# Retention states as 128x128 blocks of two heads, results as one run of whole-array matmuls into one bank

## The reference, cut to what matters

```
result[t] = (decay_matrix * (q[t] k[t]^T)) v[t]                     within the chunk, both directions
          + (decay_0 * q[t]) state[0, before t]                     what earlier chunks left
          + (decay_1 * q[t]) state[1, after t]                      what later chunks left
state[e, next] = decay_e^128 * state[e, this] + k[t]^T (weight_e * v[t])
```

## Time and profile before

| | us |
|---|---|
| median of three runs | 2710.48 |
| lowest and highest | 2708.75, 2711.12 |
| the profiled execution, by its own time | 2710.8 |
| its span in the trace | 2709.0 |
| what lies around the span | 1.8 |

### The profile page before, as it was taken

The page is one execution under the profiler, slowest core; times in us unless marked ns, Lnnn a source line. Parts: engine busy times, 40 slices in busy tenths (PEclk is TensorE's granted clock), DMA queues, the critical chain, the costliest instruction groups (busy, mean ns, idle before and its releaser), DMA issues.

```text
span 2709.0 us, 30075 instructions
## 1 busy us (share of the span) xinstructions
PE 2497.3 (92%) x12526; PEld 1757.2 (65%) x12526; DVE 1150.0 (42%) x1966; ACT 694.4 (26%) x1218; POOL 145.4 (5%) x136
## 2 busy tenths in 40 slices
PE   7987979999999998889899999999998999799997
PEld 6873433333446987735788888876756654588886
DVE  3246331211544675725243343344265473354444
ACT  2235011111222243314211211213244352312222
POOL 0000011111022003300000000000000000000000
PEclk9988979999997798999899999999999999899999
DMA  9944469997411110031111221211100100222231
GB/s 356 337 141 128 177 241 378 336 364 297 154 33 48 32 32 1 1 140 47 47 63 47 78 63 47 78 63 49 63 16 1 63 1 31 78 78 94 93 100 72
DMA packets 178791, 302.48 MB, mean 112 GB/s; under 512 B 17963, under 2 KB 89307, under 8 KB 178528
## 3 DMA queue, kind: packets, MB, share of 16 engines
q1 hardware_dynamic: 167760, 278.46, 29.7%
q0 software_dynamic: 10320, 20.00, 2.1%
q10 hardware_dynamic: 576, 2.10, 0.2%
HBM read 348.75 MB, written 18.87 MB: 136 GB/s over the span
## 4 chain that ended last, share of the span: by engine, by line
PE 52%; DVE 8%; ACT 4%; issue 2%; DVEq 0%; ACTq 0%
PE PS L135 44%; PE PS L141 4%; PE PS L147 2%; PE PS L2727 2%; DVE R L113 1%; DVE sm L116 1%; DVE X L105 1%; DVE MIX L105 1%; ACT R L125 1%; DVE rest L105 1%; DVE H L105 0%; ACT ATb L128 0%; DVE hn L105 0%; ACT ATb L125 0%; DVE sil L110 0%
## 5 line engine op out<-in xcount | busy, mean ns | idle before, releaser
L135 PE MATMUL PS<-at,wH 128*128 128x512 f32 (+1 forms) x2112 | 567.9, 357 | 4.7 <-DVE at L105 4.7
L135 PEld LDWEIGHTS PS<-at,wH 128*128 128x128 f32 x2112 | 378.2, 191 | 64.0 <-issue 7.2
L135 PE MATMUL PS<-at,rest 128*128 128x512 f32 (+1 forms) x1056 | 375.9, 356 | 0.0
L135 PE MATMUL PS<-wH,ac 128*128 128x512 f32 x880 | 278.9, 395 | 8.9 <-issue 3.9
L105 DVE TENSOR_TENSOR rest<-ring,wH 128x2048 fp32r<-128x2048 f32 x66 | 150.4, 2291 | 242.7 <-ACT wH L128 242.2
L135 PE MATMUL PS<-ring,AT 128*128 128x512 f32 x512 | 229.0, 606 | 1.7 <-ACT AT L128 1.7
L135 PEld LDWEIGHTS PS<-at,rest 128*128 128x128 f32 x1056 | 201.1, 190 | 28.4
L128 ACT CAST wH<-ring 128x2048 fp32r<-128x2048 f32 x66 | 124.7, 1906 | 316.4 <-PE PS L135 230.4
L135 PEld LDWEIGHTS PS<-wH,ac 128*128 128x128 f32 x880 | 167.3, 190 | 46.3 <-issue 8.6
L135 PEld LDWEIGHTS PS<-ring,AT 128*128 128x128 f32 x512 | 98.2, 194 | 121.3 <-issue 119.0
L135 PE MATMUL PS<-rest,ac 128*128 128x512 f32 x440 | 172.9, 393 | 0.0
(11 more groups left out here) (324 smaller groups left out, 3857.4 us busy)
## 6 DMA issues: line engine op xcount, KB each, us to landing
R<-in_w_gate_up_dram SPq DMA_DIRECT2D x32, 1024.0 KB, 12.0
ring<-in_w_down_dram SPq DMA_DIRECT2D x32, 1024.0 KB, 12.7
ring<-in_w_gate_up_dram SPq DMA_DIRECT2D x32, 1024.0 KB
ring<-in_w_ffn_gate_dram SPq DMA_DIRECT2D x22, 1024.0 KB, 5.5
ring<-in_w_ffn_up_dram SPq DMA_DIRECT2D x22, 1024.0 KB, 5.4
ring<-in_w_ffn_down_dram SPq DMA_DIRECT2D x22, 1024.0 KB, 4.9
ring<-in_w_ada_dram SPq DMA_DIRECT2D x16, 1024.0 KB, 6.8
HIw<-in_w_gate_up_dram SPq DMA_DIRECT2D x16, 1024.0 KB, 8.2
```

The lines of the kernel that those rows point to most:

```text
L135: ins = self.e.matmul(out, l, r, start=k == 0, stop=k == len(pairs) - 1)
```

## The change

- The states of a direction now alternate between two places (256 columns each), and each state is also spread by ACT into a block form (blocks): 128 partitions by 512 columns, where column block g of 128 columns is a 128x128 matrix with head 2g in its upper left, head 2g + 1 in its lower right, and zeros elsewhere. The function expand does that with two casts of 64 partitions by 256 columns for each state, and raises "expanded".
- POOL writes the zeros beforehand with three fills: three times 512 columns of MIX, 2048 columns of the ring's slot 2, and 1536 of its slot 1, each raising "zeros". The first two stand ahead of its work on q, the third ahead of the third chunk of it.
- result(i) issues its 8 matmuls of W with v in one run, and then for each direction 4 matmuls with the whole 128x128 weights of decayed q and 128 columns of blocks. All go into one bank. It waits for "expanded" instead of "state_r".
- ACT copies a result with one cast of 512 columns. The eight high parts are no longer all at the start: two come after four states are spread, two after six, two after each of the first two result copies. The first weight piece is cast after the third result copy instead of the second.
- DVE waits, before it overwrites a state's place, until that place's earlier state is spread.
- SP issues the pieces RET + 2 and RET + 3, whose slots now hold blocks, only after the last result (y_r 6).

```diff
@@ qkv_pool
+        g.wait_ge(S("dt_raw"), 2)
+        g.up(g.e.memset(MIX[:, 1024:4096].rearrange("p (t d) -> p t d", t=3)[:, :, 512:1024], 0.0), S("zeros"))
+        g.up(g.e.memset(ring[:, 4096:6144], 0.0), S("zeros"))
+
         for i, t in enumerate(YS):
             g.wait_ge(S("qk6_copy"), 8)
+            if i == 2:
+                g.wait_ge(S("proj6"), 18)
+                g.up(g.e.memset(ring[:, 2048:3584], 0.0), S("zeros"))
             if 2 <= i < 4:
                 g.wait_ge(S("kv_r"), i - 1)
@@
-    RAW_AT, Y_AT = (3, 4), ((2, 5), (6, 7))
+    RAW_AT, Y_AT = (3, 4), (2, 6)
...
     def state(e, n):
-        q = 5 * e + n
-        Z, a_ = (X, 5632 + 256 * (q - 8)) if q > 7 else (MIX, 1024 * (1, 2, 0, 3)[q // 2] + 512 + 256 * (q % 2))
-        return Z[:, a_:a_ + 256]
+        Z, a_ = ((X, 5632), (MIX, 512))[e]
+        return Z[:, a_ + 256 * (n % 2):a_ + 256 * (n % 2) + 256].rearrange("p (g d) -> p g d", g=4)
+
+    def blocks(e, n):
+        q = after_state(e, n) - 1
+        Z, a_ = (MIX, 1536 + 1024 * q) if q < 3 else (ring, 4096 + 512 * (q - 3)) if q < 7 else (ring, 2048 + 512 * (q - 7))
+        return Z[:, a_:a_ + 512]
@@ ret_pe, result(i)
-            p.wait_ge(S("state_r"), max(after_state(e, Y_STATE[e][t]) for e in ways))
-            for g in range(4):
-                outs = [bk(Y_AT[i % 2][j], 64, 64 * g) for j in range(2)]
-                for j in range(2):
-                    h = 2 * g + j
-                    p.e.matmul(outs[j], W[:, 128 * h:128 * h + 128], rv[:, t, 64 * h:64 * h + 64], start=True, stop=False)
-                for e in ways:
-                    for j in range(2):
-                        rs = slice(64 * j, 64 * j + 64)
-                        ins = p.e.matmul(outs[j], q_by(i, e)[rs, g, :], state(e, Y_STATE[e][t])[rs, 64 * g:64 * g + 64],
-                                         start=False, stop=e == ways[-1])
+            p.wait_ge(S("expanded"), max(after_state(e, Y_STATE[e][t]) for e in ways))
+            b = Y_AT[i % 2]
+
+            for h in range(8):
+                p.e.matmul(bk(b, 64, 64 * h), W[:, 128 * h:128 * h + 128], rv[:, t, 64 * h:64 * h + 64], start=h == 0, stop=False)
+            for e in ways:
+                for g in range(4):
+                    ins = p.e.matmul(bk(b, 128, 128 * g), q_by(i, e)[:, g, :], blocks(e, Y_STATE[e][t])[:, 128 * g:128 * g + 128],
+                                     start=False, stop=e == ways[-1] and g == 3)
@@ ret_act
+        def expand(a_, b_):
+            for s_ in range(a_, b_):
+                e, n, i = STATES[s_]
+                a.wait_ge(S("state_r"), s_ + 1)
+                a.wait_ge(S("zeros"), 1 if s_ < 3 else 2 if s_ < 7 else 3)
+                for j in range(2):
+                    rs = slice(64 * j, 64 * j + 64)
+                    a.cast(blocks(e, n)[rs, :].rearrange("p (g j d) -> p g j d", g=4, j=2)[:, :, j, :], state(e, n)[rs, :, :],
+                           inc=S("expanded") if j else None)
...
-        for k in range(8):
-            a.cast(aH[:, k, :], aT[:, k, :], inc=S("a_high"))
+        expand(0, 4)
+        split(0, 2)
+        expand(4, 6)
+        split(2, 4)
+        expand(6, 10)
         for i in range(6):
             copied(i)
-            if i == 1:
+            if i < 2:
+                split(4 + 2 * i, 6 + 2 * i)
+            if i == 2:
                 a.wait_ge(S("kv_r"), 6)
                 high(a, RET)
@@ ret_dve, states
+                if n > 1:
+                    v.wait_ge(S("expanded"), after_state(e, n - 2))
@@ sync
+            elif n in (RET + 2, RET + 3):
+                fetch(s, n, (S("y_r"), 6))
```

More of the change, by code:

```diff
@@ L1836, in copied, with split @@
             a.wait_ge(S("y_r"), i + 1)
-            for j in range(2):
-                a.cast(mx[:, t, 0:512].rearrange("p (g j d) -> p g j d", g=4, j=2)[:, :, j, :], bk(Y_AT[i % 2][j], 256).rearrange("p (g d) -> p g d", g=4),
-                       inc=S("y_copy_r") if j else None)
+            a.cast(mx[:, t, 0:512], bk(Y_AT[i % 2]), inc=S("y_copy_r"))
+        def expand(a_, b_):
[7 more added lines that the diff above has]
+                           inc=S("expanded") if j else None)
+        def split(a_, b_):
+            for k in range(a_, b_):
+                a.cast(aH[:, k, :], aT[:, k, :], inc=S("a_high"))
         a.wait_ge(S("params"), 128)
@@ L1857, in states @@
                 e, n, i = STATES[s_]
-                new, kv = (x.rearrange("p (g d) -> p g d", g=4) for x in (state(e, n), state(e, n)))
-                kv = bk(i % 2).rearrange("p (g e d) -> p g e d", g=4, e=2)[:, :, e, :]
+                kv = bk(i % 2).rearrange("p (g e d) -> p e g d", g=4, e=2)[:, e, :, :]
+                new = state(e, n)
+                if n > 1:
+                    v.wait_ge(S("expanded"), after_state(e, n - 2))
                 if n:
                     v.settle()
-                    v.tt(new, state(e, n - 1).rearrange("p (g d) -> p g d", g=4), bc(ET2[:, 4 * e:4 * e + 4], 64), ALU.mult)
+                    v.tt(new, state(e, n - 1), bc(ET2[:, 4 * e:4 * e + 4], 64), ALU.mult)
                 v.wait_ge(S("kv_r"), i + 1)
```

## The result

| | us |
|---|---|
| before, median of four runs | 2710.8 (2708.75 to 2713.47) |
| after, median of four runs | 2682.9 (2682.56 to 2685.82) |
| ratio, with its 95% interval | 0.9899 (0.9882 to 0.9916) |
| predicted | 2683.5, range 2679.0 to 2692.5 |
| the profiled execution after: its time, its span | 2682.56, 2679.7 |

A forecast was written before the change was run, and what follows sets the result against it. PE was taken to bound the retention results stage, at half clock. From the profiled execution, 2710.8 - 27.7 + 0.2 (POOL's fills) + 0.2 (one more hand-over) = 2683.5 us; range 2679.0 to 2692.5.

The forecast's parts named there:

- The bound: Retention's results, 856 to 905 us: PE busy 48.2 of 49 us at clock 0.50, no other engine near.
- The clock: In the new results PE's clock stays at 1.00, as in the state space stage from 1082 to 1142 us.
- a clock that stays low or goes up and down: Results stage: clock stays at 0.50, only 8.0 us gained, 2702.8 us (7%); up and down lies between (4%).
- The sum of the stage: New results and raw runs: 23.5 us plus 0.3 for turns, 23.8 us; last result ends 27.7 us earlier.
- the turn around a raw run: Into and out of each raw run between results: 0.04 x 8 = 0.3 us, bounds 0 and 1.3 us.
- my two losses of 0.2 us: POOL's third fill slowing DVE's last rotations, 0.2 us, and one more hand-over at the end, 0.2 us.
- clock changes in later stages: After retention: an us or so each way for where clock changes fall.
- DVE in the stage: Results stage: scores 1.29 us, low parts through at about 874.8, before PE ends at 876.4; costs nothing.
- ACT: Spreading states: two casts of at most 0.33 us each, 6.5 us for ten states; nothing is late.
- POOL: Three zero fills of 1.4, 1.8 and 1.4 us; the third, at about 838 us, costs 0.2 us.
- SP: RET + 2 and RET + 3 fetched from 876.4, landed by about 888; cast at 898 to 900, hidden.
- What I did not count: Projections behind the results shrink some 2.7 us at full clock, but become PE idle time behind DVE's chain.

The follow-up runs named there:

- e1_wide: The kernel before, with W's matmuls moving 128 columns instead of 64 (not for the last head), the added ones never read: 2690.9 us, ratio 0.9936.
- e5_cols16: The changed kernel with every result matmul moving 16 columns instead of 64 and 128: 2700.7 us, ratio 0.9966.
- e4_cols64: The changed kernel with the block matmuls moving 64 of their 128 columns: 2682.5 us, ratio 0.9905.
- e7_early: The changed kernel with the second weight piece's cast and low part moved ahead of the last result: 2680.4 us, ratio 0.9883; repeated, 2679.2 us.
- e2_runs: The kernel before with only the order changed, W's 8 matmuls first, then each direction's half-row matmuls: 2682.6 us, ratio 0.9909.
- e3_pairs: The changed kernel with the old order back, head pair by head pair, blocks kept: 2678.8 us, ratio 0.9898.

## Why the prediction was right

- **The bound** was right: PE, at 0.50 of its clock, in the stage of the results.
- **The clock** was right, and by the right mechanism as far as it went. The forecast took it from the nearest rows and left 11% for a clock that stays low or goes up and down. e1_wide and e5_cols16 showed what stood behind it. The forecast gave two reasons, no alternation and 128 columns over all rows in the second half. Neither is needed by itself: e1_wide has the alternation and e4_cols64 has 64 columns, both at 1.00. The Trainium skill's rule (TensorE: Matmul & The Clock Gate, the table of why this matters), to keep TensorE continuously busy, does not cover this case: 38.0 of 38 us busy at 0.50 in e5_cols16, 31.4 of 32 busy at 1.00 in e1_wide.
- **The sum of the stage** was 1.3 us too small: 23.8 forecast, 25.1 measured (873.23 + 2.00 - 850.17), and it lies above the forecast's own upper bound of 23.5 + 1.3 = 24.8. About half of the miss is the turn around a raw run. It was taken as 0.04 us, eight times. By the runs of this stage it is 0.11 out of one (852.01 - 850.17 = 1.84, against 873.23 - 871.50 = 1.73 behind a block run) and 0.09 into one (861.87 - 859.94 = 1.93, against 871.50 - 869.66 = 1.84). The first W run, behind the last kv, pays the 0.11 too. That makes 0.9 us where 0.3 was taken; the bound of 0.16 a turn held. The other half is the block runs, taken from the earlier trace rows as 0.89 and 1.78 where they measure 0.95 and 1.84 without a turn, and the last one, whose 2.00 us to the end of its last record stand against a pace of 1.78. In the kernel before, the forecast had counted that last end in.
- **What cancelled it** is luck. The forecast took 27.3 us off the profiled execution, and 28.2 came. The stage gave 1.1 us less than forecast (26.6 against 27.7), and 1.1 us more lay around the span. Against that the first kv was 2.2 us earlier in this trace, 0.2 and 0.3 us fell elsewhere, and my two losses of 0.2 us did not come. No step of mine had the 2.2 us, and they scatter by more than their size. For clock changes in later stages I allowed an us or so each way; behind the stage traces differ by some 4 us in each of two places, and the two profiled executions happened to be alike in both. The part that is surely the change's is 26.6 us.
- **DVE in the stage** was right: scores of 1.29 us, the first piece's low part through at 873.24 (forecast 874.8), 2 us before PE's last result ended. **ACT**: a spread is 0.83 us where I had at most 0.65, ten of them 8.3; PE waited for none. **POOL**: 1.38 us for the third fill, at 835.57, beside DVE's rotations, whose first two took 1.29 us as before; the 0.2 us I took for it are 0.
- **SP** was right. The cast of RET + 2 came at 899.07 (forecast 898 to 900) with the transfers done by about 883 (0.99 of the DMA in the stretch 876 to 882, idle soon after): 16 us of slack.
- **What I did not count, and rightly**: the 2.4 us that PE's projections gained at full clock became idle time, 6.33 us ahead of line 147 against 3.88 in the earlier trace rows, and the chain stayed at 58.17 us. e7_early confirmed whose chain it is, down to the 3.3 us at which the projections begin to bind.
- **What the forecast could not tell**: how much each half of the change is worth. It spoke of one stream without turns; the runs showed that the order alone (e2_runs) or the blocks alone (e3_pairs) give 26.4 and 26.6 of the 26.6 us. From before to e1_wide the clock brings 52.4 - 32.1 = 20.3 us, net of the added columns. From there to e2_runs it is 6.1 us, of which 18 x 0.06 = 1.1 are those columns and 5.0 the turns at full clock. That fits the pair: 0.95 us in the earlier trace rows against 1.73 / 4 = 0.43 for its W records and 0.94 / 4 = 0.24 for its half-row ones in long runs (16 of them take 0.94 us in e2_runs) leave 0.28 for the two turns, and 18 pairs of turns fewer are 5.0 us.

## What to carry to other kernels

Read PE's granted clock in each stretch beside its busy share: here a PE full of narrow matmuls ran at half clock for 49 us, and there everything in the stage cost nearly twice as much, the turns between half-row and whole-array matmuls too. Group matmuls by the part of the array they use before changing their data's form; here a loop's order did what blocks, zeros and 20 extra casts did. Before counting the next stage's gain, look for a distance that another engine sets: it came out the same to 0.01 us. And split a total that came out right into its stretches before trusting it: here the stage fell short and other stretches made up for it.

## What was not expected of the hardware

- Adding columns that are never read made the kernel 17 us faster (e1_wide, clock 1.00), and moving an eighth to a quarter of the columns made it 20 us slower (e5_cols16, clock 0.50), with the same number and order of matmuls each time.
- A turn between half-row and whole-array matmuls costs 0.09 to 0.11 us at full clock beside a long run (after), and 0.14 in the alternation by pairs (0.28 for two, before).
- Two half-row f32 matmuls of 64 columns, side by side, cost as much as one whole-array one of 128: 1.84 us for 32 records (e2_runs) and 1.84 for 16 (after). Padding two heads with zeros neither costs nor gains on PE by itself.
- The same kernel, unaltered, ran one stretch of 40 us at a clock of 0.87 in one trace and at 1.00 in two others, and took 4 us more in the first.
